# Levels 1 to 4 of the recurrence's triangular inverse on 32x32 diagonal blocks in four row strips, level 5 for the off-diagonal block alone

## What is computed

```python
def step(S, inp):
    w_t, k_t, v_t, kk_t, kka_t = inp[:5]
    S = (S * w_t[:, :, None, :]
         - jnp.einsum('bhij,bhj->bhi', S, kk_t)[..., None] * kka_t[:, :, None, :]
         + v_t[..., None] * k_t[:, :, None, :])
    y = jnp.einsum('bhij,bhj->bhi', S, inp[5]) if emit else None
    return S, y
...
for d, reverse in enumerate((False, True)):
    s_ctx, y_c = wkv_scan(s0, decay_c, k_dc, v_c, kk_c, a_c, r_c, reverse)
    _, y_d = wkv_scan(s_ctx, decay, k_d, v, kk, a, r, reverse)
```

## Time and profile before

| | us |
|---|---|
| median of 3 runs | 2382.73 |
| span of the profiled execution | 2385.3 |
| the recurrence's 8 chunks and its readout, about 893 to 1290 in that span | 397 |
| PE, DVE and ACT busy in those 397 | 365.5, 301.5, 177.1 |

### The profile page before, as it was taken

One profiled execution on the slowest core, in us unless ns is written; L12 is line 12 of the kernel. 1 busy time (PEld: TensorE's weight loads), 2 busy tenths in 40 slices (PEclk: granted clock), 3 DMA queues, 4 the chain that ended last, 5 costly groups with the idle time before them and its releaser, 6 DMA issues.

```text
span 2385.3 us, 46871 instructions
## 1 busy us (share of the span) xinstructions
PE 2263.7 (95%) x20728; PEld 1862.9 (78%) x20728; DVE 1452.8 (61%) x2443; ACT 1005.5 (42%) x1768; POOL 48.3 (2%) x53
## 2 busy tenths in 40 slices
PE   8999999999999999999999999998999999899997
PEld 5864478888867788899988899896677879667786
DVE  3273436867746357887774553465475876656576
ACT  2243333332313224544432464344354655444564
POOL 1000000000000000000000000020000002000000
PEclk9999999999999999999999999998999999999999
DMA  8235237756522100000002356544355863204484
GB/s 350 106 124 195 88 129 296 262 196 247 213 79 106 36 1 4 3 4 3 12 3 101 133 177 243 217 159 177 142 184 216 332 221 142 71 1 177 174 338 176
DMA packets 47307, 348.03 MB, mean 146 GB/s; under 512 B 5264, under 2 KB 5280, under 8 KB 5760
## 3 DMA queue, kind: packets, MB, share of 16 engines
q1 hardware_dynamic: 45936, 334.52, 37.6%
q0 software_dynamic: 1168, 10.51, 1.1%
HBM read 343.96 MB, written 1.05 MB: 145 GB/s over the span
## 4 chain that ended last, share of the span: by engine, by line
PE 79%; DVE 12%; ACT 6%; issue 1%; DMA 1%; DVEq 0%; ACTq 0%
PE banks L544 27%; PE banks L2210 7%; PE banks L1009 6%; PE banks L3077 3%; PE banks L3078 3%; PE banks L3079 3%; PE banks L2069 2%; PE banks L1827 2%; PE banks L609 2%; PE banks L855 2%; PE banks L3108 2%; PE banks L2287 2%; PE banks L3110 2%; PE banks L3109 2%; PE banks L556 1%
## 5 line engine op out<-in xcount | busy, mean ns | idle before, releaser
L522 DVE TENSOR_TENSOR mlp_w_low<-weight_slots,mlp_w_high 128x2048 fp32r<-128x2048 f32 x64 | 146.5, 2289 | 194.9 <-ACT mlp_w_high L513 194.9
L522 DVE TENSOR_TENSOR moe_w_low<-weight_slots,moe_w_high 128x2048 fp32r<-128x2048 f32 x96 | 217.9, 2289 | 61.9 <-ACT moe_w_high L513 61.2
L513 ACT ACTIVATE mlp_w_high<-weight_slots 128x2048 fp32r<-128x2048 f32 x64 | 122.2, 1910 | 182.7 <-PE banks L544 118.2
L513 ACT ACTIVATE moe_w_high<-weight_slots 128x2048 fp32r<-128x2048 f32 x96 | 181.7, 1914 | 23.8 <-PE banks L3110 19.7
L2210 PE MATMUL banks<-weight_slots,arena 64*64 64x64 f32 (+1 forms) x3648 | 147.3, 223 | 18.9 <-ACT arena L2230 13.3
L2210 PEld LDWEIGHTS banks<-weight_slots,arena 64*64 64x64 f32 x3648 | 139.1, 134 | 27.3 <-ACT arena L2230 15.2
L1009 PE MATMUL banks<-arena,weight_slots 128*128 128x256 f32 (+1 forms) x512 | 145.6, 440 | 3.0 <-DVE arena L2744 1.5
L1009 PEld LDWEIGHTS banks<-arena,weight_slots 128*128 128x128 f32 x512 | 99.0, 194 | 44.2 <-issue 33.6
L3077 PE MATMUL banks<-moe_w_high,slots_x 128*128 128x512 f32 x320 | 129.6, 405 | 2.8 <-DVE moe_w_low L522 2.8
L3078 PE MATMUL banks<-moe_w_low,slots_x 128*128 128x512 f32 x320 | 126.4, 395 | 0.0
L3079 PE MATMUL banks<-moe_w_high,slots_x 128*128 128x512 f32 x320 | 126.3, 395 | 0.0
(11 more groups left out here) (444 smaller groups left out, 5038.0 us busy)
## 6 DMA issues: line engine op xcount, KB each, us to landing
weight_slots<-weights SPq DMA_DIRECT2D x318, 1024.0 KB, 4.9
arena<-small POOLq DMA_DIRECT2D x1, 2560.0 KB, 9.1
arena<-x_t POOLq DMA_DIRECT2D x1, 2048.0 KB, 11.1
arena<-bias POOLq DMA_DIRECT2D x1, 2048.0 KB, 10.7
constants<-consts POOLq DMA_DIRECT2D x1, 1410.0 KB, 17.5
out_t<-arena SPq DMA_DIRECT2D x1, 1024.0 KB, 3.9
parameters<-params POOLq DMA_DIRECT2D x1, 763.0 KB, 21.3
arena<-pool_inv POOLq DMA_DIRECT2D x1, 512.0 KB, 14.5
```

Source lines behind the costliest of these rows:

```text
L513: nc.scalar.activation(self.pair(j)[0], slot(j, 0, SLOT), ACT.Copy).then_inc(*act.step("high", j))
L522: nc.vector.tensor_tensor(self.pair(j)[1], slot(j, 0, SLOT), self.pair(j)[0], ALU.subtract).then_inc(*v.step("used", j))
```

## The change

`X`, `Z` and a working copy of the inverse, now called `XB`, `ZB` and `XIB`, hold only the 32x32 diagonal blocks: 256 columns in place of 512. At levels 1 to 4 each pair has four matmuls of 32x32 by 32 columns, one for each strip of 32 partitions. The masks, transposes, seeds and copies of these levels work on 256 columns. `first_inverse` has four DVE operations in place of three: it masks all 512 columns into a scratch buffer, adds the two halves together, adds the identity and transposes.

Level 5 is replaced. `corner_inner` computes the inner product of the off-diagonal block for both directions into one bank, and a DVE copy takes it out without a mask. `second_blocks` brings the second diagonal block into place by four matmuls of 32x32 by 256 columns with the identity, and `corner_grow` makes the off-diagonal block beside it. The full `XI` is put together by ACT in two pieces for each direction: `first_block_out` after level 4, and `last_out` in place of the level 5 copy. The first half of the next chunk's `orders` for `bm` now stands between `second_blocks` and `corner_grow`, and the second half behind them. The seed of the next chunk waits for `first_block` in place of the finished inverse.

```diff
+            def inner(c, d, lv):
+                X_, BM = XB[d], bm_of(c, d)
+                b = take_bank(pe, ("z", c, d, lv), WORK_BANKS)
...
+                for p in range(PAIRS):
+                    for q in range(4):
+                        r, at_ = quarter(q), 32 * (q % 2)
+                        ins = nc.tensor.matmul(psum(b, p * 32, 32, r), BM[r, p, at_:at_ + 32], X_[r, p, :],
+                                               start=True, stop=True)
+                ins.then_inc(*pe.step("z", c, d, lv))
...
                 for p in range(PAIRS):
-                    for h in range(2):
-                        r = half(h)
-                        ins = nc.tensor.matmul(psum(b, p * 64, 64, r), Z[r, p, :], XI[r, p, :], start=False,
+                    for q in range(4):
+                        r = quarter(q)
+                        ins = nc.tensor.matmul(psum(b, p * 32, 32, r), Z[r, p, :], XI[r, p, :], start=False,
                                                stop=True, skip_group_check=True)
...
+            def corner_inner(c):
+                b = take_bank(pe, ("corner", c), WORK_BANKS)
...
+                for p in range(PAIRS):
+                    for d in range(2):
+                        for h in range(2):
+                            one, two, _, at_ = corner(d, h)
+                            ins = nc.tensor.matmul(psum(b, p * 32, 32, two), bm_of(c, d)[one, p, at_:at_ + 32],
+                                                   XB[d][one, p, :], start=True, stop=True)
+            def second_blocks(c):
+                for d in range(2):
+                    b = take_bank(pe, ("last", c, d), WORK_BANKS)
+                    pe.wait_ge(*after("inverse_t", c, d, LEVELS - 2))
+                    for h in range(2):
+                        _, two, _, at_ = corner(d, h)
+                        nc.tensor.matmul(psum(b, 0, 256, two), cn("ident64", at_, 32, two), XIB_OF[c % 2][two, d],
+                                         start=True, stop=True)
+            def corner_grow(c):
+                pe.wait_ge(*after("corner_out", c))
+                for p in range(PAIRS):
+                    for d in range(2):
+                        b = events.where["last", c, d]
+                        for h in range(2):
+                            one, two, _, _ = corner(d, h)
+                            ins = nc.tensor.matmul(psum(b, p * 32, 32, one), CORNER[two, p, :], XIB_OF[c % 2][two, d, p, :],
+                                                   start=True, stop=True)
...
+                corner_inner(c)
+                second_blocks(c)
                 if c < 7:
-                    for d in range(2):
-                        orders("bm", c + 1, d, WK["B"][:, d], "beta")
+                    orders("bm", c + 1, 0, WK["B"][:, 0], "beta")
+                corner_grow(c)
+                if c < 7:
+                    orders("bm", c + 1, 1, WK["B"][:, 1], "beta")
...
-                act.wait_ge(*after("inverse_t", c - 1, d, LEVELS - 1))
-                nc.scalar.activation(psum(INVERSE_BANKS[d]), flat(XI_OF[c % 2][:, d]), ACT.Copy).then_inc(
+                act.wait_ge(*after("first_block", c - 1, d))
+                nc.scalar.activation(psum(INVERSE_BANKS[d], 0, 256), flat(XIB_OF[c % 2][:, d]), ACT.Copy).then_inc(
...
+            def first_block_out(c, d):
+                nc.scalar.activation(XI_OF[c % 2][:, d, :, at_:at_ + 32], psum(INVERSE_BANKS[d], 0, 256).rearrange(
+                    "p (a b) -> p a b", b=32), ACT.Copy, scale=cn("first_rows", d, 1)).then_inc(*act.step("first_block", c, d))
...
+                tt(E, bm[:, :, 0:64], first, mul).then_inc(*v.step())
+                v.wait_ge(*v.own)
+                tt(XI, E[:, :, 0:32], E[:, :, 32:64], add).then_inc(*v.step())
...
-                nc.vector.transpose(flat(WK["X"][:, d]), psum(INVERSE_BANKS[d])).then_inc(*v.step("inverse", c, d, lv))
+                nc.vector.transpose(flat(XB[d]), psum(INVERSE_BANKS[d], 0, 256)).then_inc(*v.step("inverse", c, d, lv))
...
+                    if lv == LEVELS - 1:
+                        v.wait_ge(*after("corner", c))
+                        nc.vector.tensor_copy(flat(CORNER), psum(bank_of(("corner", c)), 0, 256)).then_inc(
+                            *v.step("taken", "corner", c))
```

More of the change, by code:

```diff
@@ L81, in constants @@
     for direction in range(2):
-        for lv in range(1, LEVELS):
-            a, b = (r >> lv, s >> lv) if direction == 0 else (s >> lv, r >> lv)
+        for lv in range(1, LEVELS - 1):
+            rb, sb = (i % 32)[:, None] >> lv, np.arange(32)[None, :] >> lv
+            a, b = (rb, sb) if direction == 0 else (sb, rb)
             later.append((a // 2 == b // 2) & (a % 2 == 1) & (b % 2 == 0))
-    c["later_levels"] = np.concatenate(later, 1)
+    c["block_levels"] = np.concatenate(later, 1)
     c["ident64"] = (r == s)
+    c["ident32"] = (i % 32)[:, None] == np.arange(32)[None, :]
+    c["first_rows"] = np.stack([i % 64 < 32, i % 64 >= 32], 1)
     c["scan_keep"] = np.broadcast_to(np.arange(512) % CHUNK != 0, (P, 512))
@@ L2170, in bass_two_blocks, with blocks32, quarter, corner @@
         XI_OF = [WK["XI"], slots_area(7168, 2, PAIRS, 64)]
+        def blocks32(at):
+            return ring[:, at:at + 256].rearrange("p (a b) -> p a b", b=32)
+        XB, ZB, CORNER = [blocks32(0), blocks32(256)], [blocks32(2048), blocks32(2560)], blocks32(2304)
+        assert 36352 + 512 <= SMALL + 3072
+        XIB_OF = [ring[:, 512:1024].rearrange("p (d a b) -> p d a b", d=2, b=32), area(36352, 2, PAIRS, 32)]
+        def quarter(q):
+            return slice(32 * q, 32 * q + 32)
+        def corner(d, h):
+            first, second = (0, 1) if d == 0 else (1, 0)
+            return quarter(2 * h + first), quarter(2 * h + second), 32 * first, 32 * second
         KK_FREE, KR_FREE = ([x[:, :, d * P:(d + 1) * P] for d in range(2)] for x in (KK, KR))
@@ L2332, in wkv_tensor @@
                 main = c >= 4
-                for lv in range(1, LEVELS):
+                for lv in range(1, LEVELS - 1):
                     for d in range(2):
-                        X_, BM = WK["X"][:, d], bm_of(c, d)
-                        pairs_matmul(pe, ("z", c, d, lv), lambda p, r: [(BM[r, p, 0:64], X_[r, p, :])],
-                                     ready=[("bm_out", c, d), ("inverse", c, d, lv - 1)])
+                        inner(c, d, lv)
                     if lv == 1:
@@ L2457, in wkv_scalar @@
                     for d in range(2):
-                        inverse_out(c, d, lv)
+                        if lv < LEVELS - 1:
+                            inverse_out(c, d, lv)
+                        else:
+                            last_out(c, d)
+                    if lv == LEVELS - 2:
+                        for d in range(2):
+                            first_block_out(c, d)
                     if lv in (1, 4):
@@ L2611, in first_inverse @@
                 v.wait_ge(*v.own)
-                nc.vector.transpose(flat(WK["X"][:, d]), flat(XI)).then_inc(*v.step("inverse", c, d, 0))
+                nc.vector.transpose(flat(XB[d]), flat(XI)).then_inc(*v.step("inverse", c, d, 0))
             def turned(c, d, lv):
                 v.wait_ge(*after("grown", c, d, lv))
-                nc.vector.transpose(flat(WK["X"][:, d]), psum(INVERSE_BANKS[d])).then_inc(*v.step("inverse", c, d, lv))
+                nc.vector.transpose(flat(XB[d]), psum(INVERSE_BANKS[d], 0, 256)).then_inc(*v.step("inverse", c, d, lv))
             def value_bonus(part):
```

43 lines of the change are left out of this document (31 added, 12 removed).

## The result

The changed kernel takes 2428.2 us (median of 4 runs, 2423.9 to 2429.4) against 2383.1 before (median of 4, 2382.6 to 2384.1). The ratio is 1.0186, with a 95% interval of 1.0165 to 1.0207: 45 us slower. The forecast was 2337, and the range ended at 2392. The profiled execution spans 2425.3 us, 40.0 more than the one before.

A forecast was written before the change was run, and what follows sets the result against it. PE's own work was taken to pace the recurrence (busy 365.5 of 397 us), DVE close behind. Walked savings over eight chunks came to 46.6 us: 2382.7 - 46 = 2337 us, with an 8-in-10 range of 2328 to 2392.

The forecast's parts named there:

- The price of a group: PE, levels 1 to 4: one direction's z or grow takes 0.60 us instead of 0.93; bounds 0.47 and 1.87.
- DVE and ACT: Recurrence: 256-column DVE masks and transposes take 0.42 us instead of about 0.69, ACT's inverse copies 0.37 instead of 0.60.
- Level 5: PE, level 5: 1.2 us of strips plus 0.7 for 256-column matmuls, 1.9 instead of 3.7; 1.12 mask wait goes.
- The walk: Recurrence, queues stepped forward through a chunk: chunk 2 takes 37.0 us against a walked 43.0; eight chunks save 46.6.
- rival 3: Levels 1 to 4: instruction supply limits PE, a group takes 1.2 to 1.87 us, slower, up to +95 us; 17%.
- The sum: Whole kernel: the walked saving of 46 us taken off the median of 2382.7 gives 2337 us.

The follow-up runs named there:

- one-pass run: Changed kernel with each strip of inner and grow at levels 1 to 4 reading its operands' upper 16 bits as bf16, half the instructions: 2329.3 us.
- level 5 alone: Kernel before with only a new off-diagonal level 5, added straight into the inverse's bank; levels 1 to 4 unchanged: 2371.2 us, 2367.0 on another chip.
- stream run: Kernel before with wait-free matmuls (32x32 strips, 64x64 and 128x128 tiles) added on PE after all its work: 2489.2 us.

## Why the prediction was wrong, step by step

**The price of a group: right.** 0.64 us was measured (0.60 taken). The Trainium skill's rule from "TensorE: Matmul & The Clock Gate", section "Wait — 56ns, not 53.3ns?", that matmuls start no closer than 25 ns, does not hold here: 128 records in 1.27 us are 10 ns each. The Trainium skill's section "The mechanism" on the same page, with some 4 ns between starts on different tiles, comes nearer, though the strips here do not reach it.

**DVE and ACT: right.** Their groups by line and shape, changed kernel:

```profile
L2755 DVE TENSOR_TENSOR weight_slots<-banks,constants 128x256 f32<-128x256 f32 x64 | 27.1, 424 | 76.8 <-PE banks L2307 74.9
L2718 DVE STREAM_TRANSPOSE weight_slots<-banks 128x256 f32<-128x256 f32 x64 | 28.0, 445 | 44.7 <-PE banks L2321 44.0
L2513 ACT ACTIVATE arena<-banks 128x256 f32<-128x256 f32 x32 | 12.2, 384 | 64.6 <-DVE weight_slots L2718 64.3
```

The terms were 0.42, 0.42 and 0.37.

**Level 5: mostly right.** Its 128 matmul records of strips take 1.4 us (two passes of 0.68) for the 1.2 taken, and `second_blocks` in chunk 2 of the changed kernel 0.56 (L2347, 1022.97 to 1023.53) for 0.7. In the one-pass run, where stops do not cover it, `corner_grow` never waits for DVE's copy, as I had it, but `corner_inner` waits for ACT, 3.2 us in 3. In level 5 alone, which has no `second_blocks` to cover them, both waits are there: 0.43 + 0.52 for 1.12.

**The walk: right where the supply allows it.** It gave 37.0 us for chunk 2 and ACT's copies as the first wait. With half of the instructions chunk 2 takes 37.2 and ACT holds PE for 16 us. That the numbers are so close is in part luck: a group has half of the passes there (0.3 us), and the clock is lower. The terms listed in the walk at levels 2, 3 and 4 also add up to 4.7, 4.9 and 5.7 us, and not to the 4.9, 5.3 and 6.2 that stand beside them; what the missing 1.1 us are is not said.

**The step that failed: the supply of instructions, rival 3.** The sum took a group's price from the array alone, 0.60 us, and had no term for the time in which the instructions arrive; the mechanism was named as rival 3 and given 17%. In its place the runs show stops of 78 us at steps of 256 instructions: a starved PE gets such a block only every 3.75 to 4.02 us. Two steps in the treatment of the rival were wrong.

First, the evidence against it. I said that the pace of the densest streams, 64 records in 1.86 us, is explained by columns and a little overhead, so nothing need be at a limit. Both can be true at once. The 64x64 stream of the experiment needs 3.8 us of array time for 256 instructions, and a block comes every 3.75 to 4.02 us once PE is starved. The kernel before ran right beside this limit without a wait for "issue" in the recurrence, and a change that cuts an instruction's array time from 14.5 to 5 ns (0.64 us for 128) runs into it at once. A pace that one cause explains does not show that the next limit is far.

Second, its price. I put 14.5 ns an instruction on each group, 1.87 us, all of it in the walk, and got +95 us. A block is fetched while PE does sparser work, so part of a group's instructions is there when it starts: stops included, a group took 1.3 us on average over the eight chunks. A lower bound was to be had from the number of instructions in a chunk. Chunk 1 has 1673 + 1672 = 3345, and by 14.5 ns that is 48.5 us; it took 49.5. Chunk 2: 3346, 48.5, and it took 50.2. Chunk 5: 3729, 54.1, and 58.0. Before, 1155 + 1154 = 2309 in chunk 1 were 33.5 of 43.7 us. So the count alone would have put an early chunk some 5 us above the old one and a late one near its old time: near +20 for the kernel, slower and not faster. It falls short of the +45, in the late chunks above all, because a sparse stretch stocks no more than about one block for the dense one behind it.

The sum then closes roughly. The 46 us are saved, and so are the 10 of waits that the walk had left, since PE now waits for nobody. The stops are 74 us in 893 to 1290 and 4 behind it: 2383 - 46 - 10 + 78 = 2405. The 23 us that are missing would be the work at 1.2 GHz; the trace has such passes (3.20 us for the L2230 pass at 992.66 to the next start, 1.86 before), but no run prices them by themselves, so this part is not shown.

The Trainium skill's page "Runtime: NRT & Kernel Launch", section "Instruction fetch mechanics", has the block of 256 instructions, which the count from stop to stop confirms. It also has the fetch hidden behind a floor of some 20 cycles for each instruction at issue. This floor is what the runs refute: PE took 256 in 1.27 us, 5 ns each, and then stood still for up to 2.75.

## What to carry to other kernels

Before splitting matmuls into smaller tiles, count the engine's instructions in the stage and hold the count against the time: here a starved PE got an instruction every 14 to 16 ns, and an f32 matmul of this program has four of them at every tile size. Count in blocks of 256, since a sparse stretch stocked about one block and no more. Look for idle time put down to "issue" at regular counts; the cure is not to add instructions, as level 5 alone shows, which gained 0.5% with as many as before. A stop costs only what it does not take from a wait behind it, so the place of dense work matters as well as its amount.

## What the runs showed of the hardware

- PE's instructions come in blocks of 256. Starved, PE gets a block every 3.75 to 4.02 us with strips of 32 columns and every 3.47 with strips of 64. About one block is fetched ahead: in 27 us of 64x64 matmuls at 107 ns each, without a stop, packets started 6.8 to 7.0 us apart.
- A 64x64 matmul gains nothing from fewer moving columns at 1.2 GHz: 256 of 32 columns took 27.5 us in the stream, 107 ns each, and 32 matmuls of 64 columns took 3.46 us in the changed kernel (1018.81 to 1022.27; granted clock 0.50 from 1019.2 to 1022.4), 108 ns each.
- The granted clock can stay low with PE busy all the time. Stretches of the stream run: the strips, the 64x64 matmuls of 32 columns, the strips of 64 columns.

```profile
2389.50:2418.00 28.50, 13.71 (x935) 12.73 (x935) 0.00 (x0) 0.00 (x0) 0.00 (x0) 0.57 0.02 4
2418.00:2445.00 27.00, 27.00 (x512) 27.00 (x510) 0.00 (x0) 0.00 (x0) 0.00 (x0) 0.50 0.01 3
2445.00:2458.00 13.00, 9.13 (x505) 8.59 (x507) 0.00 (x0) 0.00 (x0) 0.00 (x0) 0.88 0.02 4
```

  It fell during the strips with their stops, stayed at 1.2 GHz through 27 us of uninterrupted 64x64 work, and rose to 2.4 in the strips of 64 columns, though these had stops again.
- A wait that is already fulfilled is not free on PE: in the run with added waits each took 89 ns of the kernel's time on average, part of it at 1.2 GHz (a granted clock of 0.71 in 893 to 1500).
